# Reordering the slots of the gated DeltaNet stage: decay exponentials behind the sigmoid, inverse levels one slot later, block rows and value taps moved

## The reference, cut to what matters

```python
proj = xn @ w_in
qkv = silu(causal_depthwise_conv(proj[..., :3072], conv_w))       # 4 taps
q, k = l2norm(q) * dk ** -0.5, l2norm(k)
# chunked delta rule, per head and chunk
gam = exp(where(incl, gcum[:, None] - gcum[None, :], NEG_BIG))
a_low = where(strict, beta[:, None] * (k @ k.T) * gam, 0)
u, w = triangular_solve(eye + a_low, [v * beta, k * beta * exp(gcum)])
# recurrence over the chunks
v_new = u - w @ s
o = (q * exp(gcum)) @ s + ((q @ k.T) * gam) @ v_new
s = s * d_last + k_dec.T @ v_new
```

## Time and profile before

| | us |
|---|---|
| median of 3 runs | 3050.57 (3048.69 to 3053.46) |
| the profiled execution, its own time | 3047.07 |
| its span, first to last instruction | 3045.1 |
| PE busy, share of the span | 2592.0, 85% |
| DVE busy | 1583.1, 52% |
| ACT busy | 1122.8, 37% |
| POOL busy | 593.9, 20% |
| stage 2, first to last copy of taps (DVE line 1080) | 154.1 to 1636.6 |

### The profile page before, as it was taken

One profiled execution on the slowest core, in us unless ns is written; L12 is line 12 of the kernel. 1 busy time (PEld: TensorE's weight loads), 2 busy tenths in 40 slices (PEclk: granted clock), 3 DMA queues, 4 the chain that ended last, 5 costly groups with the idle time before them and its releaser, 6 DMA issues. The chain is left out here.

```text
span 3045.1 us, 51249 instructions
## 1 busy us (share of the span) xinstructions
PE 2592.0 (85%) x17497; PEld 2299.1 (76%) x17497; DVE 1583.1 (52%) x3692; ACT 1122.8 (37%) x3278; POOL 593.9 (20%) x509
## 2 busy tenths in 40 slices
PE   5468878798898888988989559999985999999996
PEld 5357777788888888888888428888864788778875
DVE  4256565667766766776776332222224444444443
ACT  4234444444444444443444232333323322232222
POOL 0033333311111111111111000000002323232321
PEclk8679999999999999999999669999996999999998
DMA  8763344444345344343342143333325212121211
GB/s 245 229 225 131 126 159 133 154 129 128 122 133 183 110 135 131 115 135 120 111 138 89 42 154 126 125 107 134 129 86 164 80 57 74 64 77 56 72 52 44
DMA packets 272982, 367.27 MB, mean 121 GB/s; under 512 B 74626, under 2 KB 191442, under 8 KB 272882
## 3 DMA queue, kind: packets, MB, share of 16 engines
q1 hardware_dynamic: 231762, 340.64, 34.1%
q10 hardware_dynamic: 41120, 25.37, 2.8%
HBM read 246.96 MB, written 118.98 MB: 120 GB/s over the span
## 5 line engine op out<-in xcount | busy, mean ns | idle before, releaser
L1174 PE MATMUL p_psp<-xg,p_whi 128*128 128x264 f32 x4096 | 839.2, 296 | 21.7 <-POOL p_wlo L1105 19.4
L1174 PEld LDWEIGHTS p_psp<-xg,p_whi 128*128 128x128 f32 x4096 | 660.6, 193 | 24.9 <-issue 22.6
L1174 PE MATMUL p_psp<-xg,p_wlo 128*128 128x264 f32 x2048 | 607.3, 297 | 0.0
L1174 PEld LDWEIGHTS p_psp<-xg,p_wlo 128*128 128x128 f32 x2048 | 393.7, 192 | 0.0
L952 DVE SCALAR_TENSOR_TENSOR p_acc<-p_proj,p_taps,p_acc 128x528 f32<-128x528 f32 x288 | 245.7, 853 | 9.4
L2233 PE MATMUL p_psq<-p_wq,p_hT 128*128 128x512 f32 x768 | 217.0, 421 | 37.7 <-DVE p_wq L2174 27.5
L1678 PE MATMUL p_psh<-p_wo,p_o 128*128 128x512 f32 (+1 forms) x816 | 198.9, 403 | 24.8 <-DVE p_wo L1648 21.3
L1678 PEld LDWEIGHTS p_psh<-p_wo,p_o 128*128 128x128 f32 (+1 forms) x816 | 150.0, 186 | 67.3 <-issue 20.4
L2233 PEld LDWEIGHTS p_psq<-p_wq,p_hT 128*128 128x128 f32 x768 | 140.7, 196 | 72.6 <-issue 22.1
L2233 PE MATMUL p_pso<-p_wo,p_oT 128*128 128x512 f32 x768 | 189.7, 400 | 5.1 <-DVE p_oT L2128 5.1
L973 DVE TENSOR_TENSOR p_prod<-p_Xb,p_blk 32x4 f32<-32x4 f32 (+13 forms) x448 | 187.3, 418 | 4.5
(11 more groups left out here) (265 smaller groups left out, 4792.3 us busy)
## 6 DMA issues: line engine op xcount, KB each, us to landing
p_whi<-w_dram SPq DMA_DIRECT2D x92, 512.0 KB, 4.3
p_wlo<-w_dram SPq DMA_DIRECT2D x92, 512.0 KB, 5.7
p_wraw<-w_a_in SPq DMA_DIRECT2D x36, 512.0 KB, 5.9
w_dram<-p_whi SPq DMA_DIRECT2D x34, 512.0 KB, 4.0
w_dram<-p_wlo SPq DMA_DIRECT2D x34, 512.0 KB, 5.1
xg<-xT_dram SPq DMA_DIRECT2D x8, 2112.0 KB, 13.2
hT_dram<-p_hT SPq DMA_DIRECT2D x32, 512.0 KB, 2.9
p_hT<-hT_dram SPq DMA_DIRECT2D x32, 512.0 KB, 4.2
```

The costliest lines, as they stand in the source:

```text
L1174: ins = nc.tensor.matmul(ps_p[half_][:, 0:HALF], (w_hi, w_lo)[i][:, f, kc * P:(kc + 1) * P], xg[:, g % 2, j, kc, half_ * HALF:(half_ + 1) ...
```

## The change

All of it is in `gated_deltanet`. ACT's two exponentials leave the stage `gates` and become a stage `decays` in slot 11; DVE's part of `gates` stays in slot 10. `norm` is put behind the stages of `p` in slot 12, so that on ACT it follows the squares of `tokK`. The levels and `set` move one slot later, and so do `kk`, `kdec` and `low`. Three taps of V come earlier, the rows are dealt out anew, and the products of slots 12 to 22 too. The squares of the recurrence's output get a third buffer of their own, `sq[:, 2]`. The number of instructions of each kind in a step stays as it is.

```diff
-        sq = sb("p2_sq", [P, 2, TPG, P])
+        sq = sb("p2_sq", [P, 3, TPG, P])
...
-        FILL = (8, 9, 6, 8, 9, 8, 4, 10, 8, 8, 10, 8, 3, 2, 3, 5, 2, 9, 12, 12, 13, 13, 9, 13)
-        TAPS = {7: (0, 0, (0, 1)), 8: (0, 0, (2, 3)), 9: (0, 0, (4,)), 16: (0, 1, (0,)), 17: (0, 1, (1,)),
-                18: (0, 1, (2, 3)), 19: (0, 1, (4,)), 20: (0, 2, (0, 1)), 21: (0, 2, (2, 3)), 22: (0, 2, (4,)),
+        FILL = (8, 9, 6, 8, 9, 8, 4, 10, 8, 8, 10, 8, 8, 4, 2, 5, 4, 4, 8, 13, 13, 13, 9, 13)
+        TAPS = {7: (0, 0, (0, 1)), 8: (0, 0, (2, 3)), 9: (0, 0, (4,)), 13: (0, 1, (0,)), 14: (0, 1, (1,)),
+                16: (0, 1, (2,)), 18: (0, 1, (3,)), 19: (0, 1, (4,)), 20: (0, 2, (0, 1)), 21: (0, 2, (2, 3)), 22: (0, 2, (4,)),
...
-        ROWS_P = {19: (1, 2), 20: (3,), 21: (4,), 22: (5, 6), 23: (7,)}
-        ROWS_A = {0: (8, 9), 1: (10,), 2: (11,), 3: (12,), 4: (13,), 5: (14,), 6: (15,)}
+        ROWS_P = {20: (1, 2), 21: (3,), 22: (4, 5), 23: (6,)}
+        ROWS_A = {0: (7, 8), 1: (9,), 2: (10,), 3: (11,), 4: (12, 13), 5: (14,), 6: (15,)}
...
-                put(12, "norm", main, 0)
...
-                    put(12 + 2 * level, "left", main, level)
-                    put(13 + 2 * level, "right", main, level)
-                put(18, "set", main, 0)
+                    put(13 + 2 * level, "left", main, level)
+                    put(14 + 2 * level, "right", main, level)
+                put(19, "set", main, 0)
...
-                for s, stage in ((12, "tokK"), (13, "kk"), (13, "kdec"), (14, "low"), (22, "tokV"), (23, "vs")):
+                    put(11, "decays", q, 0)
+                for s, stage in ((12, "tokK"), (14, "kk"), (14, "kdec"), (15, "low"), (22, "tokV"), (23, "vs")):
...
+            if b:
+                put(12, "norm", b[-1], 0)
...
-                if stage == "gates":
+                if stage == "decays":
...
-                    nc.scalar.activation(sq[:, 0, index, :], o_of(p, index), ACT.Square,
+                    nc.scalar.activation(sq[:, 2, index, :], o_of(p, index), ACT.Square,
```

## The result

| | before | changed |
|---|---|---|
| median of 4 runs, us | 3052.02 (3048.69 to 3057.46) | 2985.42 (2976.61 to 2987.34) |
| profiled execution, us | 3047.07 | 2984.5 |
| its span, us | 3045.1 | 2982.5 |

The ratio is 0.9763, with a 95% interval of 0.9743 to 0.9784: 66.6 us faster by the medians.

What follows compares the result with a forecast made beforehand. PE, busy 85% of the span, bounds the kernel through its waits and clock falls. Plain steps 30 + meta 16 + first steps 4 + clock 20 = 70 us off 3047.07 gives 2977, median 2980; own range 2962 to 2995, overall 2955 to 3022.

Steps and rivals of the forecast that it cites:

- Plain steps of about 42.9 us: Sign that the forecast is right: plain steps this long in place of the 44 to 44.3 of most.
- Decays behind the sigmoid: ACT's two exponentials after the sigmoid: 1.5 us off the path to the silu of K in plain steps, 2.1 in meta.
- Order of level 0 and K's transposes: PE idles 1.2 us before K's transposes, then runs level 0 after them; the plain step's wait for the inverse's DMA goes.
- The 1.3 us of a plain step: Net gain per plain step: 1.45 us from 12 more products before right of level 2, less 0.1 to 0.2.
- The 0.45 us expected before right of level 2: PE's wait there in plain steps, with four products in front of it instead of two.
- The bound of 2.2 us: Most a plain step could gain: PE's waits 0.24 + 1.40 + 0.54, called four waits, with nothing left.
- Clock: 20 us from falls of PE's granted clock given back: six in meta steps, 15 us; two of three in plain, 5.
- the inference that the clock holds: Meta wait for K falls from 3.73 to 1.6 us, no more than a plain step's 1.64, where the clock holds.
- Meta steps: Six steps x 2.7 = 16 us, from 2.1 by the decays and 0.6 in the levels; clock falls 15 us besides.
- Rival 1: Waits shrink but the clock stays low behind the 1.6 us left: gain 50 us, 3000; chance 0.22.
- Rival 3: V's taps on DVE land whole on the level chain if ACT's half 3 copy is late: slower, 3072; chance 0.06.
- Rival 4: DVE's taps copy slips ahead of POOL, cutting 1.2 us of `p_r` wait every second step: 13 us, 2967; chance 0.07.

Runs made afterwards that it cites:

- the late copy: The changed kernel with DVE's copy of 12 tap columns moved from the step's start to slot 5: 2957.53 us, ratio 0.9686 to the kernel before.
- the last run above: The kernel before with only DVE's copy of 12 tap columns moved to slot 5: 3067.03 us, ratio 1.0046 to the kernel before.

## Why the prediction was right, and where it was off

The time, the main mechanism and most of the signs named in advance are there: the wait for K at 1.2 to 1.3 us in plain and 1.7 in meta steps, no wait for the inverse's DMA, the wait for `p_r` still at 1.9 us. Two are not. "Plain steps of about 42.9 us" holds for half of them only; 11 of 22 take 44.0 or more. And `p_X` makes PE wait before left of level 2 in five meta steps, 1.2 us in all. In the profiled executions 62.6 us of span came off where 70 were forecast.

*Decays behind the sigmoid:* right. 1.5 us off K's path were forecast; the change by this part alone takes 44.25 - 42.75 = 1.5 us off a plain step and carries 53 of 66.6 us.

*Order of level 0 and K's transposes:* right in its mechanism. A wait of 1.2 us was forecast and 1.3 is there, and the DMA wait is gone. But in plain steps this order brings no gain of its own, since the clean step is the same with level 0 inside the wait. What the other parts bring beside the decays lies mostly in step 16 and in the steps up to 9. The levels and the dealt-out products were never run by themselves, so their share is not shown.

*The 1.3 us of a plain step:* a little too small, 44.25 - 42.78 = 1.47 us, 32 us over 22 steps where 1.3 makes 29. The 0.45 us expected before right of level 2 is 0.29, and the 0.2 before left of level 2 is not there. The bound of 2.2 us speaks of four waits and adds three: the 0.41 before right of level 1 is missing, and it went, as did the 0.2 for the state, which the sum did not have either.

*Clock, the term that was mis-sized.* Of its 20 us, 15 were for six meta falls and 5 for two of three falls in plain steps. In the meta steps five came back whole and the sixth in part (0.86 over 12 us), and a new one stands behind `p_r` (0.79 over 8 us, from 350 us). In plain steps the three falls went: steps 16, 25 and 26 take 42.7 or 42.8 us. But falls came up behind the wait for `p_r` in 11 steps, at 1.3 us each. 988.5 - 22 x 44.25 = 15 us lay above the clean steps before, and 956.3 - 22 x 42.78 = 15 us do now: net zero instead of 5.

The step that failed is the inference that the clock holds behind a wait of no more than 1.64 us, because it held in step 17. Steps 10, 11 and 27 of the kernel before took 45.9 us each and were not in the count. Step 11 stood still for 0.76 + 0.88 = 1.64 us, as long as step 17 with its 0.24 + 1.40; behind it the clock fell, in step 17 it held:

```profile
757.18 1.10 PE L1233 MATMUL p_psl<-p_X,p_nU 128*128 128x64 f32 x8 [0.76 <-DMA p_Xt<-inv_dram]
759.17 0.88 PE L1192 MATMUL p_psk<-p_ident,p_kT 128*128 128x128 f32 x4 [0.88 <-POOL p_kT L1124]
...
759.17:767.17 8.00, 7.60 (x51) 7.41 (x52) 3.39 (x12) 3.94 (x19) 1.28 (x1) 0.79 0.58 203
1030.30:1038.30 8.00, 7.58 (x64) 7.24 (x65) 4.24 (x13) 3.94 (x19) 1.28 (x1) 1.00 0.73 223
```

*Meta steps:* 16 + 4 + 15 = 35 us forecast, 31.1 measured up to step 9. Left out were the wait for `p_kdec` of the meta pass (0.5 us a step), 0.3 us more for `p_vs` and up to 0.3 for `p_X`; the sum had 0.6 us of gain in the levels in their place.

*Rivals.* Rival 1, that the clock does not come back, named the right danger in the wrong steps. By the rule of the Trainium skill, "TensorE: Matmul & The Clock Gate", section "Part 4: PE-mode transpose", that transposes do not count as busy in the same way, the time would have been this rival's. This trace does not bear it out: the clock is 1.00 in five of six meta steps with the transposes right behind the wait. Rival 3, the thin place, came closer than forecast: the V tap was to end 0.1 us before the addition to `p_X` was due and ends 0.07 behind that point. It cost nothing in plain steps, because level 1 starts 0.57 us after the addition. Rival 4, the copy in front of POOL, did not come, by a margin of 0.03 us that nobody had planned; the 0.14 us of before had shrunk by 0.1:

```profile
964.66 1.27 DVE L1082 COPY p_taps<-p_convw 128x12 f32 x1 [0.29 <-DVE p_Xb L977]
...
964.63 1.27 POOL L1126 TENSOR_TENSOR p_qT<-p_acc,p_sig 128x512 f32<-128x512 f32 x1 [4.82 <-ACT p_sig L842]
```

The copy began 0.03 us behind POOL and ended 0.03 us behind it. This agrees with the Trainium skill, "SBUF — State Buffer", section "Who interferes with whom": the later one blocks until the first is done. Where the rows stand was worth at most 5 us; the forecast put nothing there.

What stays open is what decides at which of several short waits the clock falls.

## What to carry to other kernels

Ask of each instruction on the path what stands in front of it on its own engine and is not needed yet: two exponentials of 0.6 us ahead of a sigmoid cost 1.5 us in each plain step, and one copy of 12 columns made a wait 1.3 us longer. Do not count such a wait as won before the next link is looked at: of these 1.3 us, 0.9 came back behind the rows, and the step became some 0.5 us shorter. Reordering one engine's queue pays only where the engine that waits has work to put in the gap, so move both together, and price the rare steps apart from the common ones. And give every wait two prices, its own length and a possible fall of the clock: with the late copy the second was about as large as the first, and twice falls came up behind another wait when one was shortened.

## What the runs showed of the hardware that was not expected

The clock falls behind waits much shorter than the 3.3 to 3.7 us of the earlier trace rows, and the length of a wait does not decide it alone. In the kernel before, 1.64 us of standing still had 0.79 behind it in step 11 and 1.00 in step 17. In the changed kernel waits of 1.8 to 1.9 us for `p_r` have 0.79 over 8 us in 11 of 22 plain steps and 1.00 in the other 11. With all but the decays changed, a wait of 2.75 us has 0.79 behind it at 1046 us, and 14 later waits of 2.75 to 2.9 us have 1.00:

```profile
1046.40:1054.40 8.00, 8.00 (x55) 7.84 (x56) 2.92 (x7) 3.35 (x18) 1.28 (x1) 0.79 0.58 193
1092.50:1100.50 8.00, 8.00 (x69) 7.82 (x70) 4.50 (x14) 3.95 (x19) 1.28 (x1) 1.00 0.47 180
```

A fall recurs at the same slot for several steps in a row, in the last run above in nearly every plain step, in a smaller and a larger size by turns (45.3 and 46.8 us). With the late copy in the changed kernel it stays away over 22 steps. The 22 plain steps take 15 us more than 22 clean ones in the kernel before and in the changed one, and 1010.9 - 22 x 43.39 = 56 us more in the last run above.

DVE and POOL are coupled by more than semaphores. A DVE copy of 12 columns per partition takes 0.17 us, or 1.27 us if it is issued 0.03 us behind the start of a POOL multiplication of 1.27 us; issued 0.4 us behind, it takes 0.9. In all 22 plain steps of the changed kernel it ends 0.03 or 0.04 us behind POOL's. A product of 32x64 elements takes 0.26 us in the changed kernel and 1.22 with the late copy, where it is issued 0.18 us behind the start of `p_qd`.
